# Splitting weights for exact products: fewer, larger VectorE operations in an MLP step, a finer wait at its entrance, and a weight chunk that arrives in halves

## The reference

```python
h = rmsnorm(x, g_mix);  proj = h @ w_in          # 5120 columns: q,k,v twice, two gates
y_a = moba_attention(...) @ w_br_moba            # 8 heads of 64, ALiBi, causal
y_b = stick_breaking_attention(...) @ w_br_sb    # 8 heads of 64
x = x + (sigmoid(gate_a) * y_a + sigmoid(gate_b) * y_b) @ w_out
x = x + cross_attention(rmsnorm(x, g_cross), rmsnorm(mem, g_mem), w_xq, w_xkv, w_xo)
u = rmsnorm(x, g_mlp) @ w_up                     # 1024 -> 4096
x = x + square(relu(u)) @ w_down                 # 4096 -> 1024
return rmsnorm(x, g_final)
```

## Time and profile before

| | |
|---|---|
| median of 3 runs | 413.68 us (413.5 to 413.97) |
| the profiled execution | 414.61 us, its span 412.8 us |
| TensorE matmul busy | 403.2 us, 98% of the span |
| VectorE busy | 333.6 us, 81% |
| ScalarE busy | 250.0 us, 61% |
| GpSimd busy | 28.5 us, 7% |
| granted TensorE clock, mean | 0.995 of full speed |

### The profile page before, as it was taken

How to read it: one execution, slowest core, us unless ns; L and a number is a source line. 1 busy time by engine, 2 the same in 40 slices (tenths; PEclk the granted TensorE clock), 3 DMA queues, 4 the chain that set the end, 5 groups by cost and what they waited for, 6 DMA issues and landing times.

```text
span 412.8 us, 7093 instructions
## 1 busy us (share of the span) xinstructions
PE 403.2 (98%) x2857; PEld 371.7 (90%) x2857; DVE 333.6 (81%) x441; ACT 250.0 (61%) x295; POOL 28.5 (7%) x40
## 2 busy tenths in 40 slices
PE   8999999999999999999999999999999999999992
PEld 8999988999999999889988899999999999999981
DVE  4689556967765737874858888999999999999986
ACT  6664337864665634551556648777777777777753
POOL 0059400000000000000200000000000000000003
PEclk9999999999999999999999999999999999999997
DMA  8999564534325255555453245555655566555002
GB/s 282 420 421 398 213 203 137 181 125 173 110 101 198 103 205 204 199 183 175 157 176 131 102 143 194 201 199 206 209 207 198 204 213 203 202 203 222 2 0 102
DMA packets 12107, 77.47 MB, mean 188 GB/s; under 512 B 1328, under 2 KB 1328, under 8 KB 3632
## 3 DMA queue, kind: packets, MB, share of 16 engines
q1 hardware_dynamic: 12080, 77.09, 51.6%
HBM read 76.04 MB, written 1.05 MB: 187 GB/s over the span
## 4 chain that ended last, share of the span: by engine, by line
PE 52%; DVE 22%; issue 17%; ACT 3%; DMA 3%; SPq 1%; DVEq 0%; POOL 0%; POOLq 0%; ACTq 0%
PE bank L1154 17%; PE bank L1179 16%; PE bank L1299 11%; DVE w_lo L707 5%; DVE t_lo L707 5%; DVE t_sum L950 4%; DMA raw<-in_weights_dram 3%; DVE t_sum L957 3%; PE bank L1311 1%; DVE forms L1014 1%; DVE res L1087 1%; SPq L332 1%; DVE forms L1024 1%; DVE forms L1019 1%; PE bank L1404 1%
## 5 line engine op out<-in xcount | busy, mean ns | idle before, releaser
L707 DVE TENSOR_TENSOR w_lo<-raw,w_hi 128x2048 fp32r<-128x2048 f32 (+2 forms) x83 | 145.3, 1756 | 26.4 <-ACT w_hi L455 25.2
L1154 PE MATMUL bank<-hT_hi,w_hi 128*128 128x256 f32 x386 | 107.0, 278 | 0.6 <-DVE hT_lo L719 0.4
L1154 PE MATMUL bank<-hT_lo,w_hi 128*128 128x256 f32 x384 | 106.3, 277 | 0.0
L1154 PE MATMUL bank<-hT_hi,w_lo 128*128 128x256 f32 x384 | 106.2, 277 | 0.0
L455 ACT ACTIVATE w_hi<-raw 128x2048 fp32r<-128x2048 f32 x33 | 62.9, 1916 | 29.4 <-PE bank L1154 13.9
L1154 PEld LDWEIGHTS bank<-hT_hi,w_hi 128*128 128x128 f32 x386 | 72.4, 188 | 1.1 <-issue 0.6
L1154 PEld LDWEIGHTS bank<-hT_lo,w_hi 128*128 128x128 f32 x384 | 72.3, 188 | 0.1
L1154 PEld LDWEIGHTS bank<-hT_hi,w_lo 128*128 128x128 f32 x384 | 72.1, 188 | 0.0
L707 DVE TENSOR_TENSOR t_lo<-t_sum,t_hi 128x1024 fp32r<-128x1024 f32 x30 | 36.5, 1218 | 0.0
L1299 PE MATMUL bank<-hT_hi,w_hi 128*128 128x256 f32 x128 | 35.8, 279 | 0.0
L1299 PE MATMUL bank<-hT_lo,w_hi 128*128 128x256 f32 x128 | 35.4, 277 | 0.0
(11 more groups left out here) (206 smaller groups left out, 856.1 us busy)
## 6 DMA issues: line engine op xcount, KB each, us to landing
raw<-in_weights_dram SPq DMA_DIRECT2D x65, 1024.0 KB, 4.8
head_all<-in_triples_dram SPq DMA_DIRECT2D x6, 384.0 KB, 6.5
raw<-in_chunk_dram SPq DMA_DIRECT2D x2, 512.0 KB, 8.2
res<-in_x_dram SPq DMA_DIRECT2D x2, 512.0 KB, 13.0
mem_tok<-in_mem_dram SPq DMA_DIRECT2D x1, 1024.0 KB, 13.0
memT_raw<-in_memT_dram SPq DMA_DIRECT2D x1, 1024.0 KB, 11.2
out_dram<-xs SPq DMA_DIRECT2D x2, 512.0 KB, 2.6
gfin<-in_g_final_dram SPq DMA_DIRECT2D x1, 512.0 KB, 5.6
```

The lines of the kernel that those rows point to most:

```text
L707: return nc.vector.tensor_tensor(dst, whole, high.bitcast(fp32), sub)
L1154: last = mm(outs[m][:, tok], w, v[:, k0 + k, tok], start=first and n == 0 and not t, stop=k == nk - 1 and n == 2, skip_group_check=bool(kt ...
```

## The change

Three edits.

1. **Chunk 3 in halves.** `CHUNK2` becomes `HALVES` and covers chunks 2 and 3, each as two DMAs of 512 KB from an input laid out for them, without gaps in the source. ScalarE and VectorE split chunk 3 in two 1024-wide operations each. On TensorE chunk 3 gets a wait per half, and by that the order k outer, m inner; `spread_rstd` stands in front of tile (6, 1), the fourteenth.
2. **up(0) waits by part.** `up_first` replaces up(0): for each k it waits for hT_hi only, issues high x high and low weight x high for both m, and waits for hT_lo ahead of the last two of six matmuls. up(0) writes bank 6 instead of bank 0.
3. **VectorE's list.** The two `low_down` of a step (1024 and 512 wide) become one of 1536, which waits for `t_made` = 3u+3; `low_t13` and `low_t24` become `low_t`, 2048 wide, at the end of the list. The same in step 0. TensorE's waits count accordingly.

```diff
-            load(3, 3)
+            for i, (c, k0, k1) in enumerate(HALVES):
+                sp.dma_start(raw[:, c, k0 * SEQ:k1 * SEQ], chunk23[i]).then_inc(half_in[i], 16)
...
-            split(3)
+                dve.wait_ge(*((piece_hi, first_half(c)), (w_hi_ready, c + 1))[i % 2])
+                low(w_lo[:, c, cols], raw[:, c, cols], w_hi[:, c, cols]).then_inc((piece_lo, w_lo_ready)[i % 2], 1)
...
-            def low_t13(u, i=0):
+            def low_t(u, i=0):
 
                 dve.wait_ge(t13_hi, PER * i + (u + 1))
...
                 dve.wait_ge(t24_hi, PER * i + (u + 1))
...
+                low(t_lo[:, u % 2, :], t_sum[:, u % 2, :], t_hi[:, u % 2, :]).then_inc(t_lo_done, 1)
...
             def mlp_rest(u, i=0):
                 low_up(u + 1, i)
                 sum_t4(u, i)
-                low_down(u, B11, B22 + 1, 3 * u + 2, i)
-                low_t13(u, i)
+                low_down(u, B11, B21 + 1, 3 * u + 3, i)
                 form_s31(u, i)
-                low_down(u, B21, B21 + 1, 3 * u + 3, i)
                 form_s2(u, i)
-                low_t24(u, i)
                 form_s4(u, i)
+                low_t(u, i)
...
-            low_down(0, B11, B22 + 1, 2)
-            low_t13(0)
-            low_down(0, B21, B21 + 1, 3)
-            low_t24(0)
+            low_down(0, B11, B21 + 1, 3)
+            low_t(0)
...
-                          halved=(0, 1, 0) if c == 3 else None)
+                          halves_of_chunk(c) if c <= 3 else None,
+                          (lambda: spread_rstd(X_ROW_BANK, 1)) if c == 3 else None, (KT - 2, 1),
+                          halved=(KT - 2, 1, 0) if c == 3 else None)
...
+            def up_first():
+
+                c, outs = up_chunk(0), halves(UP_BANK(0))
+                pe.wait_ge(up_lo, 1)
+                for k in range(KT):
+                    pe.wait_ge(hi_done[X2], k + 1)
+                    for n, (w, v) in enumerate(((w_hi[:, c % RING, :], hT_hi), (w_lo[:, c % RAW, :], hT_hi),
+                                                (w_hi[:, c % RING, :], hT_lo))):
+                        if v is hT_lo:
+                            pe.wait_ge(lo_done[X2], k + 1)
...
-            up(0, kt_wait=lambda k: pe.wait_ge(lo_done[X2], k + 1))
+            up_first()
```

More of the change, by code:

```diff
@@ L55, in weight_chunks, with hybrid_layer @@
     return cols, at
-def hybrid_layer(nc, x, head0, head1, pair, triples, chunk2, mem, memT, g_final, weights, ff, out):
+def hybrid_layer(nc, x, head0, head1, pair, triples, chunk23, mem, memT, g_final, weights, ff, out):
     fp32, f32r = mybir.dt.float32, mybir.dt.float32r
@@ L113, in hybrid_layer, with first_half @@
     FIRST, PAIR, HEAD_PIECES = 2, 2, KT + 1
-    CHUNK2 = [(0, 4), (4, 8)]
+    HALVES = [(c, k0, k0 + 4) for c in (2, 3) for k0 in (0, 4)]
+    def first_half(c):
+        return HEAD_PIECES + c - 2
     def piece_of(k):
@@ L483, in _ @@
                 head_high(k)
-            for i, (k0, k1) in enumerate(CHUNK2):
+            for i, (c, k0, k1) in enumerate(HALVES):
                 cols = slice(k0 * SEQ, k1 * SEQ)
                 act.wait_ge(half_in[i], 16)
-                copy(w_hi[:, 2, cols], raw[:, 2, cols], ACT.Copy).then_inc((piece_hi, w_hi_ready)[i], 1)
-            split(3)
+                copy(w_hi[:, c, cols], raw[:, c, cols], ACT.Copy).then_inc((piece_hi, w_hi_ready)[i % 2], 1)
             act.wait_ge(x_in[0], 16)
@@ L766, in _ @@
                 head_low(k)
-            for i, (k0, k1) in enumerate(CHUNK2):
+            for i, (c, k0, k1) in enumerate(HALVES):
                 cols = slice(k0 * SEQ, k1 * SEQ)
-                dve.wait_ge(*((piece_hi, HEAD_PIECES), (w_hi_ready, 3))[i])
-                low(w_lo[:, 2, cols], raw[:, 2, cols], w_hi[:, 2, cols]).then_inc((piece_lo, w_lo_ready)[i], 1)
-            split(3)
+                dve.wait_ge(*((piece_hi, first_half(c)), (w_hi_ready, c + 1))[i % 2])
+                low(w_lo[:, c, cols], raw[:, c, cols], w_hi[:, c, cols]).then_inc((piece_lo, w_lo_ready)[i % 2], 1)
             dve.wait_ge(x_in[1], 16)
@@ L1145, in weights_T @@
                         kt_wait(k)
-                    if between and (k, m) == (0, 1):
+                    if between and (k, m) == at_:
                         between()
-                    at_ = k * cols + m * P
-                    wh, wl = w_hi[:, c % RING, at_:at_ + P], w_lo[:, c % RAW, at_:at_ + P]
+                    a = k * cols + m * P
+                    wh, wl = w_hi[:, c % RING, a:a + P], w_lo[:, c % RAW, a:a + P]
                     first = k == 0 and (m == 0 or not kt_wait)
@@ L1231, in _, with halves_of_chunk, wait @@
                 head_products([(0, k), (1, k)], piece_of(k) + 1, last=k == KT - 1)
-            def chunk2_halves(k):
-                if k % 4 == 0:
-                    pe.wait_ge(*((piece_lo, HEAD_PIECES), (w_lo_ready, 3))[k // 4])
+            def halves_of_chunk(c):
+                def wait(k):
+                    if k % 4 == 0:
+                        pe.wait_ge(*((piece_lo, first_half(c)), (w_lo_ready, c + 1))[k // 4])
+                return wait
             def spread_rstd(b, n):
@@ L1244, in _ @@
                     pe.wait_ge(row_ready, 1)
-                weights_T(c, hT_hi, hT_lo, 0, KT, halves(c), c + 1 if c > 2 else None,
-                          chunk2_halves if c == 2 else None,
-                          (lambda: spread_rstd(X_ROW_BANK, 1)) if c == 3 else None,
-                          halved=(0, 1, 0) if c == 3 else None)
+                weights_T(c, hT_hi, hT_lo, 0, KT, halves(c), c + 1 if c > 3 else None,
+                          halves_of_chunk(c) if c <= 3 else None,
+                          (lambda: spread_rstd(X_ROW_BANK, 1)) if c == 3 else None, (KT - 2, 1),
+                          halved=(KT - 2, 1, 0) if c == 3 else None)
             def scores(p):
@@ L1440, in up @@
                     pe.wait_ge(u_relu, PER * i + u)
-                weights_T(up_chunk(u), hT_hi, hT_lo, 0, KT, halves(UP_BANK(u)), None, kt_wait,
-                          halved=(0, 1, 0) if u == 0 else None)
+                weights_T(up_chunk(u), hT_hi, hT_lo, 0, KT, halves(UP_BANK(u)), None)
+            def up_first():
[7 more added lines that the diff above has]
+                            pe.wait_ge(lo_done[X2], k + 1)
+                        for m in range(2):
+                            a = k * SEQ + m * P
+                            for t in (range(TOK) if (k, m, n) == (1, 0, 0) else (None,)):
+                                tok = slice(0, SEQ) if t is None else slice(t * P, t * P + P)
+                                last = mm(outs[m][:, tok], w[:, a:a + P], v[:, k, tok], start=(k, m, n) == (0, 0, 0),
+                                          stop=(k, n) == (KT - 1, 2), skip_group_check=True)
+                last.then_inc(w_used, 1)
             def down(u, i=0, start=False):
@@ L1469, in down_plain @@
                 wh, wl = w_hi[:, c % RING, :], w_lo[:, c % RAW, :]
-                pe.wait_ge(down_lo, 2 * u + 2)
+                pe.wait_ge(down_lo, u + 2)
                 pe.wait_ge(f_lo_done, u + 1)
```

23 lines of the change are left out of this document (8 added, 15 removed).

## The result

Six runs of each kernel: before 413.59 us (413.07 to 413.97), after 416.74 (416.08 to 417.4), a ratio of 1.0071 with a 95% interval of 1.0054 to 1.0087. **The change makes the kernel slower by some 3 us.** The forecast was 416.2 in 414.5 to 417.2, slower with a chance of 0.88. The profiled execution of after took 417.39, with a span of 415.3.

What follows compares the result with a forecast made beforehand. VectorE was taken to pace MLP steps 1 to 14. Head -0.5, entrance -0.13 and fourteen steps +3.2 gave +2.5 to +2.6 us, so 413.68 + 2.5 = 416.2 us, range 414.5 to 417.2.

Steps and rivals of the forecast that it cites:

- What bounds the kernel: MLP steps 1 to 14: VectorE's twelve-operation list sets the pace, with TensorE's own list estimated at 10.25 us.
- Merges: VectorE's list: merged low_down saves 0.06 and merged low_t 0.07, together -0.13 us a step.
- Neighbour pairs: VectorE's list: three operations directly behind the one they wait for cost 0.12 each, +0.36 us a step.
- Rival A: MLP loop: a wait on the neighbour costs nothing, TensorE paces at about 10.25, total 412.5 us; chance 0.08.
- the middle case: MLP steps: only the forms' pairs cost, +0.9 us in all, total 414.6; chance 0.03.
- B: MLP loop: each neighbour wait also exposes semaphore preparation, a pair costs 0.16, total 417.9 us; chance 0.04.
- Fourteen steps: MLP steps 1 to 14: +0.23 us each, the step becomes 10.52, +3.2 us in all.
- Entrance: MLP entrance: merges in step 0 give -0.13 us; up_first's 0.4 becomes a longer wait before down(0), worth 0.
- Head: Head: the pause before chunk 3 (-0.31) and the row sum's wait (-0.2) go, -0.5 us.
- rival C: Head: its gain doesn't come, halves late or chunk 4 the next wait, total 416.7 us; chance 0.07.
- an earlier S4: MLP steps: S4 and f_hi ready some 2 us earlier, worth nothing as f_lo still follows low_t and sum_t13.
- Outside the span: Whole kernel: 1.8 us around the span in the profiled execution; differences were taken to carry over to the median.

Runs made afterwards that it cites:

- pairs0: The changed kernel with VectorE's list reordered so no operation waits for the one right ahead, merged operations kept; 413.33 us, ratio 0.9988 to before.
- the ladder: Four kernels with the same merged operations and 0, 1, 2 or 3 neighbour pairs per step; periods 10.152, 10.279, 10.405 and 10.528.
- up_only: The kernel before with edit 2 alone, up(0) waiting by part and writing bank 6; 413.85 us, ratio 1.0006.
- head_only: The kernel before with edit 1 alone, chunk 3 in halves; 413.84 us, ratio 1.0004.
- waits_swapped: The changed kernel with the two waits of low_down in the other order, t_made first; one execution took 417.78 us.
- pairs2: The changed kernel with low_t between S2 and S4, two neighbour pairs per step; 415.42 us, ratio 1.0043 to before.
- forms_together: The kernel before, nothing merged, only S31, S2 and S4 put next to each other; 417.62 us, ratio 1.0098.
- best: The changed kernel with pairs0's order, step 1 listed as in before, chunk 3 m outer, row sum ahead of tile (4, 1); 412.37 us, ratio 0.9971 to before.
- after_again: The changed kernel measured once more beside the kernel before; 416.43 us, ratio 1.0072.
- list_only: The kernel before with edit 3 alone, chunk 3 and up(0) as before; 417.27 us, ratio 1.0090.
- best_whole: The kernel best with chunk 3 in one piece again; 413.15 us, ratio 0.9983 to before.

## Why the prediction was right

**What bounds the kernel.** Right. TensorE's own step was estimated at 10.25 from a wait of 0.04 in the joint between the products; pairs0 shows 10.24. That VectorE's list was only 0.05 longer is what makes the change so uneven: a shorter list can win 0.05 a step, a longer one loses all of it.

**Merges.** Forecast 0.13 a step, measured 0.14. A reading beside it was off without harm: t_lo is done 2.3 ahead of the down product that reads it (311.02 and 313.30 in after), not "a good 3".

**Neighbour pairs.** Forecast 0.12 each from three rows outside the loop, measured 0.123 to 0.127 inside it, and nearly alike for all three. The step of the sum that carried most, +0.23 a step, measured 0.235. Rival A and the middle case fall with the ladder, B with the period: 10.53 and not over 10.6. Extra work at a wait, as B supposed, showed only where an entry of its own waits on the neighbour, 0.07 to 0.09, and after has that in steps 1 and 14 alone. A wait for an operation further back was free in pairs0, one for the neighbour was not. The Trainium skill, page "VectorE: DVE Perf Modes", section "The DRAIN you can't avoid", has a semaphore after each operation costing nothing extra, and its rules for authors count operations only. By that rule these kernels with one set of operations would take the same time; their periods, 10.15 to 10.53, disagree. Every operation raises its semaphore in all four, so what they price is the wait on the neighbour, and not the raising.

**Fourteen steps.** +3.2 forecast, +3.42 in the profiles: the two written-out steps cost 0.065 more each for the separate entry in the queue, and twelve cost 0.005 more each. This was a term slightly mis-sized; the prediction took one form of wait for all steps, though rows 4, which are written-out code, couldn't show a second wait on the same operation.

**Entrance.** Right in both parts: -0.13 measured, and `up_first` is worth nothing, since up_only shows no difference.

**Head.** In the profiled execution -0.50, as forecast, but in part by luck: the pause is 0.32 of it, as reckoned, chunk 3 itself became 0.25 shorter, of which the row sum's wait is only a part and the slower pace takes some back, and chunk 2 began 0.07 later. As a forecast of the median it was the step that failed, though not by enough to move the result out of the range: head_only shows no difference. The pause of rows 7 was taken for a property of the kernel on the word of one execution, without its spread over others. The measured 416.74 is the number of rival C, 416.7, but C's mechanism isn't seen: in after, chunk 3 and chunk 4 both begin without a pause.

**The end.** Not foreseen: -0.40 behind the last matmul. In before, ScalarE's last f_hi of the loop's kind waits for S4, and everything it does behind that is late:

```profile
392.55 0.96 ACT L642 ACTIVATE f_hi<-forms 128x896 fp32r<-128x896 f32 x1 [1.88 <-DVE forms L1024]
...
398.26 0.96 DVE L707 TENSOR_TENSOR f_lo<-forms,f_hi 128x768 fp32r<-128x768 f32 x1 [0.91 <-ACT f_hi L642]
...
403.10 3.38 DVE L1087 SCALAR_TENSOR_TENSOR res<-bank,rstd,res 128x512 f32<-128x512 f32 x5
```

VectorE starts f_lo(15) 6.63 ahead of the last matmul (404.89) and trails it with five additions back to back. In after, S4 is early, f_hi doesn't wait, f_lo(15) has 7.28, and the last addition waits for TensorE and not the other way round:

```profile
393.12 0.96 ACT L644 ACTIVATE f_hi<-forms 128x896 fp32r<-128x896 f32 x1
...
400.42 0.96 DVE L709 TENSOR_TENSOR f_lo<-forms,f_hi 128x768 fp32r<-128x768 f32 x1 [0.91 <-ACT f_hi L644]
...
408.20 0.75 DVE L1077 SCALAR_TENSOR_TENSOR res<-bank,rstd,res 128x512 f32<-128x512 f32 x1 [0.21 <-PE bank L1487]
```

The prediction had written that an earlier S4 "is worth nothing", and looked only at the steps, not at what follows the last. Over the profiles a lead of 6.63 to 6.67 goes with an end of 7.91 to 7.96, and one of 7.03 or more with 7.55 to 7.57; waits_swapped (7.29 and 7.91) is the exception, where VectorE's very last multiplication came 0.37 later behind GpSimd's rstd than in after. The nearest to a test is pairs2, which is after with S4 behind low_t again: f_hi waits for S4, the lead is 6.64 and the end 7.95, as in before. But a late S4 isn't enough for a late end, since in pairs0 f_hi waits for it too and the lead is 7.03. No run changed this by itself, so the cause is read, not tested.

**Outside the span.** The prediction let the difference of the spans carry over to the whole. But the time around the span is 1.8 in before and 2.1 in after, +0.4. Without it the medians would differ by 2.3 to 2.8, as the spans do. The two terms that were not foreseen, this and the end, cancel (+0.4, -0.4); what is left of the miss, +2.7 to +3.15 measured against +2.5 to 2.6 forecast, is the steps' 0.2 and the part of the head's 0.5 that came in some executions only. That the total came so near owes something to that cancelling.

## What to carry to other kernels

On an engine that sets the pace, count joints as well as operations: put something independent between an operation and the one that needs it, and merge only where that doesn't push dependent neighbours together. Before an operation is moved on the path, measure how far the next engine's own period is away, since that is all a saving can bring. A pause on a load in one trace is worth what it costs on average over several executions, so look at more than one before counting it.

## What the runs showed of the hardware

- **A wait on the neighbour on VectorE** costs 0.123 to 0.127, alike behind 512, 256 and 128 columns: independent neighbours start some 0.08 ahead of the end, dependent ones some 0.03 behind it. If the wait on the neighbour stands as an entry of its own in the queue, that adds 0.07 to 0.09; an entry for something long done adds nothing.
- **Matmuls of 256 columns in the head** are 0.118 apart in eight profiles, in which chunk 2 starts at 17.1 or later, and 0.113 in five, in which it starts at 16.9 or sooner, at a granted clock of 1.00 in both. Over the head that makes 0.4. A pace of 0.118 ends behind the pause in front of chunk 3 where there is one, else behind the row sum in chunk 3; from there on it is 0.113 in all thirteen. What sets it stays open.
- **The time outside the span** is 1.7 to 1.8 in before, forms_together, head_only, up_only, best and waits_swapped, and 2.0 to 2.15 in after, after_again, pairs0 to pairs2, list_only and best_whole. On the chip of the last three kernels both values stand side by side (2.12, 2.15 and 1.78), so it isn't the chip; what in a program sets it stays open. It is 0.4 of the 3 us here, about as large as the forecast's term for the head.
- **The start of chunk 2** lies between 15.9 and 17.5 in thirteen profiles of the same head pieces: executions differ by more in when their first megabytes land than the head edit could win.
